# Three token chunks as the innermost loop: consecutive matmuls of an item go to different PSUM banks

## The reference

```python
z = rmsnorm(h, norm_g)
proj = jnp.einsum('btd,de->bte', z, w_in)                     # nine groups of 1024 columns
a_val, a_glu, a_gate, b_h, b_c, b_b, b_gate, m_a, m_b = jnp.split(proj, SPLIT_IDX, axis=-1)
c_a = layernorm(causal_dwconv(buf_a, a_val * sigmoid(a_glu), conv_a_w) + conv_a_b)   # width 31
y_a = silu(c_a) * silu(a_gate)
y_b = b_b * causal_dwconv(buf_b, b_c * b_h, conv_b_w) * silu(b_gate)                 # width 3
merged = sigmoid(m_a) * (y_a @ w_pa) + sigmoid(m_b) * (y_b @ w_pb)
h = h + merged @ w_out
y = rmsnorm(h, final_norm_g)                                  # and the new convolution states
```

## Time and profile before

| | us |
|---|---|
| median of the 2 timed runs | 1141.42 |
| lowest and highest of them | 1140.95, 1141.89 |
| span of the profiled execution | 1139.5 |
| PE busy in it (6868 matmuls) | 1122.1 |
| PEld busy (6868 weight loads) | 1096.9 |
| DVE busy | 629.0 |
| ACT busy | 240.0 |
| POOL busy | 147.3 |

### The profile page before, as it was taken

One profiled execution on the slowest core, in us unless ns is written; L12 is line 12 of the kernel. 1 busy time (PEld: TensorE's weight loads), 2 busy tenths in 40 slices (PEclk: granted clock), 3 DMA queues, 4 the chain that ended last, 5 costly groups with the idle time before them and its releaser, 6 DMA issues.

```text
span 1139.5 us, 17651 instructions
## 1 busy us (share of the span) xinstructions
PE 1122.1 (98%) x6868; PEld 1096.9 (96%) x6868; DVE 629.0 (55%) x890; ACT 240.0 (21%) x326; POOL 147.3 (13%) x70
## 2 busy tenths in 40 slices
PE   6999999999999999999999999999999999999997
PEld 5999999999999999999999999999999999998885
DVE  6568787877778877788785743002222223442223
ACT  7211111111110212111111322112323231122121
POOL 2000000000000000000031212121212123442220
PEclk9999999999999999999999999999999999999999
DMA  7211211102111121211112321131111113441221
GB/s 253 67 48 37 62 56 42 52 22 78 37 42 55 31 67 37 61 42 51 37 38 74 89 62 55 55 92 57 42 50 42 50 37 131 149 147 37 111 92 58
DMA packets 101806, 75.34 MB, mean 66 GB/s; under 512 B 2735, under 2 KB 95279, under 8 KB 101764
## 3 DMA queue, kind: packets, MB, share of 16 engines
q1 hardware_dynamic: 101780, 74.97, 21.2%
HBM read 66.31 MB, written 9.63 MB: 67 GB/s over the span
## 4 chain that ended last, share of the span: by engine, by line
PE 97%; DVE 1%; ACT 1%; DMA 1%; issue 0%; SPq 0%
PE ps L1017 88%; PE ps L1192 8%; PE ps L1208 1%; DMA c<-in_x_prompt_dram 1%; DVE c L714 1%; ACT ua L462 0%; DVE z_lo L705 0%; PE spare L1135 0%; PE spare L1033 0%; PE spare L1090 0%; DVE t L714 0%; DVE t L991 0%; ACT sq L672 0%; ACT w_hi L442 0%; PE spare L1081 0%
## 5 line engine op out<-in xcount | busy, mean ns | idle before, releaser
L1017 PE MATMUL ps<-z_hi,w_hi 128*128 128x344 f32 (+2 forms) x1728 | 557.0, 322 | 0.9 <-DVE z_lo L705 0.9
L1017 PE MATMUL ps<-z_hi,w_lo 128*128 128x344 f32 (+2 forms) x1728 | 556.2, 322 | 0.0
L1017 PE MATMUL ps<-z_lo,w_hi 128*128 128x344 f32 (+2 forms) x1728 | 554.7, 321 | 0.0
L1017 PEld LDWEIGHTS ps<-z_hi,w_hi 128*128 128x128 f32 x1728 | 326.2, 189 | 2.2 <-DVE z_lo L705 1.6
L1017 PEld LDWEIGHTS ps<-z_lo,w_hi 128*128 128x128 f32 x1728 | 325.7, 189 | 0.2
L1017 PEld LDWEIGHTS ps<-z_hi,w_lo 128*128 128x128 f32 x1728 | 325.7, 189 | 0.0
L442 ACT ACTIVATE w_hi<-raw 128x1024 fp32r<-128x1024 f32 x82 | 86.8, 1059 | 580.6 <-PE ps L1017 565.5
L384 POOL TENSOR_TENSOR w_lo<-raw,w_hi 128x1024 fp32r<-128x1024 f32 x35 | 90.9, 2598 | 848.9 <-ACT w_hi L442 848.9
L765 DVE SCALAR_TENSOR_TENSOR sq<-ua,cst,sq 128x513 f32<-128x513 f32 x224 | 151.3, 747 | 0.0
L1017 PE MATMUL ps<-y_hi,w_hi 128*128 128x344 f32 x384 | 122.9, 320 | 0.0
L1017 PE MATMUL ps<-y_lo,w_hi 128*128 128x344 f32 x384 | 122.7, 319 | 0.0
(11 more groups left out here) (123 smaller groups left out, 667.6 us busy)
## 6 DMA issues: line engine op xcount, KB each, us to landing
raw<-in_w_in_dram SPq DMA_DIRECT2D x72, 512.0 KB, 3.6
t<-in_x_prompt_dram SPq DMA_DIRECT2D x9, 512.0 KB, 3.2
merged_b_spill<-t SPq DMA_DIRECT2D x8, 516.0 KB, 3.0
t<-merged_b_spill SPq DMA_DIRECT2D x8, 516.0 KB, 3.9
raw<-in_w_pb_dram SPq DMA_DIRECT2D x8, 512.0 KB, 4.0
raw<-in_w_pa_dram SPq DMA_DIRECT2D x8, 512.0 KB, 4.2
raw<-in_w_out_dram SPq DMA_DIRECT2D x8, 512.0 KB, 4.6
out_dram<-t SPq DMA_DIRECT2D x8, 512.0 KB, 2.6
```

The costliest lines, as they stand in the source:

```text
L1017: last = nc.tensor.matmul(ps[s][:, ch, 0:width], w[:, s, k, :], x[:, k, lo_col:hi_col], start=(k == 0 and n == 0), stop=(k == K - 1 and n ...
```

## The change

`item` no longer calls `chunk`. Its loops are turned inside out: k outermost, then the three parts, then the three chunks. Three consecutive matmuls now have the same stationary operand and write to three different banks. The 72 matmuls, and the order of the 24 that accumulate in each bank, stay what they were. `chunk_done` is still raised three times for an item, now by the item's last three matmuls. `chunk` stays for the first two items.

```diff
             def item(s, hi, lo, off, width):
-                for ch in range(CHUNKS):
-                    chunk(s, hi, lo, off, width, ch)
+                for k in range(K):
+                    parts = ((w_hi, hi), (w_hi, lo), (w_lo, hi))
+                    for n, (w, x) in enumerate(parts):
+                        for ch in range(CHUNKS):
+                            lo_col, hi_col = off + ch * width, off + (ch + 1) * width
+                            mm = nc.tensor.matmul(ps[s][:, ch, 0:width], w[:, s, k, :], x[:, k, lo_col:hi_col],
+                                                  start=(k == 0 and n == 0), stop=(k == K - 1 and n == 2))
+                            if k == K - 1 and n == 2:
+                                mm.then_inc(chunk_done, 1)
```

## The result

The changed kernel takes 1151.34 us (two runs, 1150.69 and 1151.98) where the kernel before takes 1141.42: ratio 1.0088, 95% interval 1.0066 to 1.0109. It is slower by 9.9 us, less than the 2% that count here as a difference, and 3.7 us above the 1147.6 of the prediction. That is inside the 1138 to 1157 us that the prediction gives with a small shift of the distances, and just above the 1145 to 1151 of the forecast by itself. The profiled execution is the slower of the two, 1151.98, with a span of 1150.2 us against 1139.5: 10.7 us more.

The account below looks back on a forecast made before the run. The prediction took PE's matmul count times the distance between matmuls as the bound. Profiled span 1139.5 + 5.0 pause + 1.2 clock = 1145.7; with timed runs 1.9 above the span, 1147.6 us, range 1145 to 1151, or 1138 to 1157 with the small shift.

Parts of the forecast that it names:

- a small shift of the distances: Rival, changed loops: operands step through other addresses and distances scatter, 9 us either way, 1138 to 1157 us; chance 0.12.
- What bounds the kernel: Whole kernel: time is the number of matmuls times their distance (0.158 us for 344 columns), plus start and end.
- The bank, priced at 0: Changed loops, 6192 matmuls: going to another bank neither saves nor costs time; 0, with 9 us either way.
- The stationary operand, priced at 0: Changed loops: three matmuls in a row with the same weights save no load and shorten no distance; 0.
- The distances, priced at 0 with 9 us either way: Changed loops: distance between matmul starts stays, keeping 0.0015 us either way for each of 6192, 9 us.
- The pause, 5.0 us: Hand-over from phase 4 to output tiles: chunk 0 is done later, so PE stands still; 5.0 us, none hidden.
- the hop: Hand-over to the output tiles: passing the finished low part on to PE takes 0.1 to 0.2 us.
- The clock, 1.2 us with bounds of 0 and 3.3: Output start: the clock may fall in PE's pause, so output begins at half speed; 1.2 us, between 0 and 3.3.
- The rest of phase 4, cost 0: Phase 4: later merging delays loads behind the spilled branch by 1.8 to 3.2 us, but slack covers it; 0.
- The cover: Phase 4: weights ready at 972.24, wanted at 979.8; 2 us left even with 3.2 us delay and one POOL operation more.
- a bank conflict goes: Rival, changed loops: a wait for the same bank disappears, 84 us faster, to 1064 us; chance 0.08.
- alternation breaks the stream: Rival, changed loops: pauses on coming back to a bank drop the clock, 82 us slower, to 1230 us; chance 0.05.

Follow-up runs that it names:

- the two runs with banks and operands apart: Against the kernel before: new operand order with old bank order, 1144.37 us; old operand order with alternating banks, all chunks done at the item's end, 1148.92 us.
- the other runs of the table above: Kernel before with only phase 4's last item in the new order, 1148.56 us; with alternating banks, old operand order, 1148.92; changed kernel with 1048-column rows, 1151.15.
- the shorter rows: Kernel before with rows of `z_hi` and `z_lo` 1048 instead of 1050 columns apart: 1139.71 us, ratio 0.9987.

## Why the prediction was right, point by point

**What bounds the kernel.** Right: in every run here the time is that of PE's distances, and of the pause; only with 2-byte parts does PE wait once more, 0.4 to 0.5 us for DVE. The part of a distance that its columns do not explain was set a little low, at 13 ns: with 344 columns it is 158.0 - 143.3 = 14.7.

**The bank, priced at 0.** Right, and more closely than could be known: the 172 changes of bank in the trace of before gave 0.0003 us with a scatter ten times as large, the two runs with banks and operands apart give 0.00001. The open point, an accumulating matmul right after a change of bank, made no difference.

**The stationary operand, priced at 0.** Right; 6868 loads stayed, and the distance of z with 344 columns too. Where distances grew, the repeat is not parted from the addresses.

**The distances, priced at 0 with 9 us either way.** This is the largest miss of the sum: 3.0 us where it has 0. The profiled span lies 4.5 us above the 1145.7 of the prediction: 3.0 from here, 1.65 from the clock, less 0.2 from the pause. The 3.0 us are inside the 9 that were kept, and the last of the rivals had them ("the distance shifts a little", chance 0.12); what that rival names, the operands' addresses, fits the runs but is not proved by them. It came together with the forecast, and without it the time would lie well inside 1145 to 1151. So two terms of the sum were too small, and it is the wider range that held the time.

**The pause, 5.0 us.** Measured 4.81. Each step of the sum is in the chain: the multiply begins 0.48 us after chunk 0's last matmul (0.46 was taken), and from there to the first output matmul it is 4.80 us (5.0 with the hop).

**The clock, 1.2 us with bounds of 0 and 3.3.** The mechanism is right, and the size is not: 2.85 us in the profiled execution. The step that failed is "nearer to zero, since the fall would be only just due". It rests on the one fall on record, 4.5 us after PE's last matmul; here the fall came after 3.8 us, and in the other runs of the table above after 2.0 to 3.2. And once it has fallen, the clock doesn't return with the first matmul but 4.2 to 6.0 us later. All four executions lost more than 1.2 us and less than the bound of 3.3 that the earlier trace rows gave.

**The rest of phase 4, cost 0.** Right in the end, with a size off. The timelines of DVE, SP and POOL in the changed kernel answer to the earlier trace rows:

```profile
971.36 0.52 DVE L966 TENSOR_TENSOR c<-ps,c 128x344 f32 x1 [6.30 <-PE ps L1028]
971.91 2.46 DVE L968 TENSOR_TENSOR c<-c,t 128x344 f32 x1
...
974.83 2.19 DVE L968 TENSOR_TENSOR c<-c,t 128x344 f32 x1
...
978.02 0.33 SPq L302 DMA_DIRECT2D t<-merged_b_spill  x1
...
973.96 2.68 POOL L406 TENSOR_TENSOR w_lo<-raw,w_hi 128x1024 fp32r<-128x1024 f32 x1
```

Two adds of this item meet POOL's work, not one, and take 2.46 and 2.19 us; its load of the spilled branch starts at 978.02, 6.8 us after the item's last matmul (at about 971.2) instead of 1.5 before. The delay is 5.3 us where 1.8 to 3.2 were reckoned for an item (for the first item the load starts at 965.09, 3.7 us late). The cover held all the same: the weights that POOL finishes at 976.64 are wanted at 982.6, at the end of the next item.

**The rivals.** That a bank conflict goes is refuted: the excess it was to remove belongs to how the operands are read. The Trainium skill, page "TensorE: Matmul & The Clock Gate", section "Back-to-back issue gap", gives N/2.4 + 2.5 ns, and calls it the gap of an isolated matmul. In the unbroken streams here the trace agrees with it where the operands are 2-byte numbers side by side (145.9 ns measured, 145.8 by the page; 215.7 and 215.8 for 512 columns), and not with the 4-byte operands of this kernel (158.0 and 231.1). That alternation breaks the stream is refuted too: the pieces of PE stay unbroken, with one pause, which alternating banks don't cause. The same page's section "A second HAM failure mode: psum-queue depth-cycling" tells of PE idling as a kernel cycles through banks; no run here shows that.

**What beats both kernels.** The order of before with 2-byte parts, 1059.23 us, 7.2% below before, at the price of fewer bits in each part. With the arithmetic left as it is, the shorter rows, 1139.71 us, by 0.13%.

## What to carry to other kernels

Before you change an order for the sake of banks, look for the places where the trace already changes bank, and compare the distance of starts there with that inside a bank. When loops are turned inside out, ask first which partial results become ready later, and who was living off the early ones: here one item at a phase's end cost 7.3 of some 10 us. And price a pause of the matrix engine together with the slow clock after it: here a pause of 4.7 us brought it in every profile that had one, for 1.3 to 2.9 us more.

## What the runs showed of the hardware

- Alternating between three banks with every matmul, against 24 in a row into one: 158.39 ns both times, for accumulating matmuls of 344 columns.
- The distance between matmuls of 344 columns is 145.9 ns with 2-byte operands side by side, 153.4 with 2-byte operands in every second place, 158.0 with 4-byte ones, all at a granted clock of 1.00. At the half level the 4-byte operands cost nothing extra: 0.29 us for 350 columns and 0.427 for 512 (mean over twelve distances after the pause), which is 350/1.2 and 512/1.2.
- Rows of the moving operand 1048 instead of 1050 columns apart move the distance by -1.2 ns (344 columns) and +0.8 (350). The order of the operands moves it by up to 1.6 ns (158.29 to 159.91 with 346 columns), whatever the banks.
- A stationary operand used three times in a row is loaded three times: 6868 loads in both kernels.
- After a pause of 4.7 us on PE the granted clock was at half, in four profiled executions out of four; it fell 2.0 to 3.8 us after PE's last matmul and came back 4.2 to 6.0 us after the restart. With 28 matmuls in the pause it stayed at 1.00.
